# A residual norm by a product with a diagonal: three norms of a two-layer float32 kernel on Trainium2

## What is computed

```python
def rmsnorm(x, g):
    xf = x.astype(jnp.float32)
    y = xf * lax.rsqrt(jnp.mean(xf * xf, axis=-1, keepdims=True) + RMS_EPS)
    return (y * g.astype(jnp.float32)).astype(x.dtype)
...
    h = rms_norm(x, norm_mix_g)
    aq, ak, av, hq, hf, hi, hg, ga, gh = split_combined(h @ w_in)
...
    x = x + merged @ w_out
    x = x + peer_layer(rms_norm(x, norm_ffn_g), w_peer_q, peer_keys, peer_u, peer_v)
```

## Time and profile before

| | us |
|---|---|
| median of 3 runs | 1443.85 |
| lowest, highest | 1443.55, 1445.56 |
| the profiled execution | 1443.56 |
| its span, first to last instruction | 1441.8 |
| TensorE busy | 1422.6 |
| VectorE busy | 967.4 |
| ScalarE busy | 738.5 |
| GpSimd busy | 212.7 |

### The profile page before, as it was taken

The page is one execution under the profiler, slowest core; times in us unless marked ns, Lnnn a source line. Parts: engine busy times, 40 slices in busy tenths (PEclk is TensorE's granted clock), DMA queues, the critical chain, the costliest instruction groups (busy, mean ns, idle before and its releaser), DMA issues.

```text
span 1441.8 us, 25221 instructions
## 1 busy us (share of the span) xinstructions
PE 1422.6 (99%) x10281; PEld 1290.2 (89%) x10281; DVE 967.4 (67%) x1752; ACT 738.5 (51%) x1066; POOL 212.7 (15%) x122
## 2 busy tenths in 40 slices
PE   8999999999999999999999999999999999999997
PEld 7989989999999999998777778888899788899986
DVE  5565674693944777778888876655577864677754
ACT  5674654545454444444444445544567754655543
POOL 5000000488883000000000000000114100000000
PEclk9999999999999999999999999999999999999999
DMA  6433456455555545445545466555543453455552
GB/s 241 142 132 125 138 157 216 141 186 180 187 180 182 170 162 174 164 164 173 174 164 174 164 222 245 181 185 188 175 147 118 159 177 112 154 188 185 181 190 103
DMA packets 67219, 245.07 MB, mean 170 GB/s; under 512 B 7456, under 2 KB 7712, under 8 KB 66848
## 3 DMA queue, kind: packets, MB, share of 16 engines
q1 hardware_dynamic: 66960, 243.19, 50.5%
q10 hardware_dynamic: 144, 0.26, 0.0%
HBM read 242.37 MB, written 1.05 MB: 169 GB/s over the span
## 4 chain that ended last, share of the span: by engine, by line
PE 77%; issue 14%; DVE 4%; ACT 4%; POOL 1%; DMA 0%; POOLq 0%; SPq 0%; DVEq 0%; ACTq 0%
PE bank L433 76%; ACT A L1154 2%; DVE wlo L1712 1%; ACT whi L1154 1%; PE bank L442 1%; DVE A L1712 1%; ACT L1154 1%; DVE A L1708 0%; DVE xres L1712 0%; DMA xres<-in_x 0%; POOL wlo L2555 0%; ACT hTh L1154 0%; DVE small L2361 0%; DVE small L1712 0%; POOL small L2561 0%
## 5 line engine op out<-in xcount | busy, mean ns | idle before, releaser
L1712 DVE TENSOR_TENSOR wlo<-raw,whi 128x1024 fp32r<-128x1024 f32 (+1 forms) x375 | 458.1, 1223 | 334.3 <-ACT whi L1154 333.9
L1154 ACT ACTIVATE whi<-raw 128x1024 fp32r<-128x1024 f32 (+1 forms) x450 | 472.9, 1053 | 401.3 <-PE bank L433 401.3
L433 PE MATMUL bank<-hTh,whi 128*128 128x256 f32 x1944 | 555.5, 286 | 2.0 <-DVE wlo L1712 1.3
L433 PE MATMUL bank<-hTl,whi 128*128 128x256 f32 x1944 | 548.6, 282 | 0.0
L433 PE MATMUL bank<-hTh,wlo 128*128 128x256 f32 x1944 | 548.0, 282 | 0.0
L433 PEld LDWEIGHTS bank<-hTh,whi 128*128 128x128 f32 x1944 | 367.0, 189 | 5.9 <-DVE wlo L1712 2.1
L433 PEld LDWEIGHTS bank<-hTh,wlo 128*128 128x128 f32 x1944 | 366.0, 188 | 0.0
L433 PEld LDWEIGHTS bank<-hTl,whi 128*128 128x128 f32 x1944 | 365.5, 188 | 0.3 <-issue 0.2
L433 PE MATMUL bank<-whi,hTh 128*128 128x512 f32 (+2 forms) x552 | 218.4, 396 | 0.2
L433 PE MATMUL bank<-wlo,hTh 128*128 128x512 f32 (+2 forms) x552 | 215.0, 390 | 0.0
L433 PE MATMUL bank<-whi,hTl 128*128 128x512 f32 (+2 forms) x552 | 214.9, 389 | 0.0
(11 more groups left out here) (178 smaller groups left out, 1391.8 us busy)
## 6 DMA issues: line engine op xcount, KB each, us to landing
raw<-in_u SPq DMA_DIRECT2D x128, 512.0 KB, 3.3
raw<-in_v SPq DMA_DIRECT2D x128, 512.0 KB, 3.3
raw<-in_w_up SPq DMA_DIRECT2D x44, 512.0 KB, 3.3
raw<-in_w_down SPq DMA_DIRECT2D x22, 512.0 KB, 3.2
raw<-in_w_in_t SPq DMA_DIRECT2D x17, 512.0 KB, 3.4
raw<-in_w_in_g SPq DMA_DIRECT2D x16, 512.0 KB, 3.3
raw<-in_w_out SPq DMA_DIRECT2D x16, 512.0 KB, 4.0
raw<-in_w_pq SPq DMA_DIRECT2D x16, 512.0 KB, 3.5
```

Source lines behind the costliest of these rows:

```text
L433: return e.matmul(o, l, r, start=st, stop=sp_, skip_group_check=True)
L1154: return e.activation(o, i, func, **kw)
L1712: return e.tensor_tensor(o, a, b, op)
```

## The change

The scalings of the three norms go. In their place ScalarE writes `diag[:, 0:128]` = `ident` times the factor of block 0 (`diag0`) and VectorE `diag[:, 128:256]` for block 1 (`diag1`), and TensorE multiplies each 128x128 tile of `xres` itself, as the stationary operand, by that diagonal: the output is the tile transposed and scaled. ScalarE adds its two partial sums of block 1 itself (`n_part`), and VectorE adds the rest and the epsilon in one operation. On ScalarE the exponential for `h_kinv` moves one step later, and the logarithms of the recurrence's norm one step later, with what follows them; on VectorE the low part of `yhT` moves one step later. In cross attention the transposes of block 1 move from the step of block 0 to the middle of the next unit. At the end GpSimd multiplies first and takes both factors after. A line of "..." stands for context that is left out.

```diff
@@ -140,20 +140,20 @@
 PARTS = {0: 1, 3: 2, 4: 3}
-SCALED = (0, 6, 10, 18, 26, 34)
-SCALED0 = {1: 2, 5: 6}
+SCALED = (0, 0, 0, 8, 16, 24)
+HEADS = {0: 1, 1: 2, 5: 3}
 B_TAPS = (2, 0, 0, 3, 6, 7, 7, 6)
...
 hi lo_dve lo_pool w acc0 acc1 acc2 ev_act ev_dve
-n_sq n_sum n_rstd n_scaled n_scaled0 n_tr n_hi n_lo r_add r_part final half
+n_sq n_sum n_rstd n_scaled n_diag0 n_diag1 n_tr n_hi n_lo r_add r_part final half
 sig lb_dve lb_act at_bias at_pe at_act at_dve hi_ev hg_pe hg_act hg_dve mg_sum mg_hi mg_lo
...
 ff_a ff_c ff_g ff_h ff_lo
-own_act own_dve own_pool zeros x_sq hi_half lo_half lo_first f_xg f_xd f_act hd_mask
+own_act own_dve own_pool zeros x_sq hi_half lo_half lo_first f_xg f_xd f_act n_part hd_mask
 """.split()
@@ -212,6 +212,7 @@
         small = sb("small", 256)
+        diag = sb("diag", 2 * P)
         with ExitStack() as c:
@@ -467,37 +468,24 @@
-            def norm_tile(j, src, b, k):
-                if k % 2 == 0:
-                    if b == 0 and j in SCALED0:
-                        e.wait_ge(s["n_scaled0"], SCALED0[j] + k // 2 + 1)
-                    else:
-                        e.wait_ge(s["n_scaled"], SCALED[j] + (4 * b if j not in SCALED0 else 0) + k // 2 + 1)
+            def norm_tile(j, b, k):
+
+                if k == 0:
+                    e.wait_ge(s[("n_diag0", "n_diag1")[b]], HEADS[j])
                 o = (k // 4 * 2 + b) * P
-                ins = tr(banks[k % 4][:, o:o + P], src[:, b * D + k * P:b * D + (k + 1) * P])
+                ins = mm(banks[k % 4][:, o:o + P], xres[:, b * D + k * P:b * D + (k + 1) * P], diag[:, b * P:(b + 1) * P])
                 if b:
...
-            def first_head(src, spins):
-
-                def tile(b, k):
-                    if k % 2 == 0:
-                        if b == 0 and k < 4:
-                            e.wait_ge(s["n_scaled0"], k // 2 + 1)
-                        else:
-                            e.wait_ge(s["n_scaled"], k // 2 - 1 if b == 0 else 3 + k // 2)
-                    o = (k // 4 * 2 + b) * P
-                    ins = tr(banks[k % 4][:, o:o + P], src[:, b * D + k * P:b * D + (k + 1) * P])
-                    if b:
-                        ins.then_inc(s["n_tr"], 1)
+            def first_head(spins):
...
                 for k in range(8):
-                    tile(0, k)
+                    norm_tile(0, 0, k)
                 spin(spins[1], 7)
                 for k in range(4):
-                    tile(1, k)
+                    norm_tile(0, 1, k)
                 spin(spins[2], 7)
@@ -505,7 +493,7 @@
                     if k < 4:
-                        tile(1, k + 4)
+                        norm_tile(0, 1, k + 4)
                     if k == 4:
@@ -525,7 +513,7 @@
-            def norm_head(j, src, u0, spins):
+            def norm_head(j, u0, spins):
@@ -533,7 +521,7 @@
                             use(k)
-                        norm_tile(j, src, b, k)
+                        norm_tile(j, b, k)
                 bk = 4 + pair[0] % 3
@@ -543,7 +531,7 @@
                             if k < 4:
-                                norm_tile(j, src, 1, k + 4)
+                                norm_tile(j, 1, k + 4)
                         ins = three(banks[bk][:, 256 * i:256 * i + 256], [z[:, k, :] for z in wv],
@@ -958,6 +946,20 @@
+            def cross_turn(h2, b):
+                e.wait_ge(s["cr_dve"], 6 * h2 + 2 * b + 2)
+                use(2 + b)
+                for a in range(2):
+                    for q in range(2):
+                        ins = tr(banks[2 + b][:, (2 * a + q) * P:(2 * a + q + 1) * P],
+                                 p2[:, 2 * h2 + b, q, a * P:(a + 1) * P])
+                ins.then_inc(s["cr_pe"], 1)
+                free[2 + b] = (s["cr_act"], 6 * h2 + 3 + b)
+
+            def turn_mid(h2):
+                cross_turn(h2, 1)
+                yield
+
             def cross_mid(h2):
@@ -970,15 +972,8 @@
                     yield
-                    for b in range(TB):
-                        e.wait_ge(s["cr_dve"], 6 * h2 + 2 * b + 2)
-                        use(2 + b)
-                        for a in range(2):
-                            for q in range(2):
-                                ins = tr(banks[2 + b][:, (2 * a + q) * P:(2 * a + q + 1) * P],
-                                         p2[:, 2 * h2 + b, q, a * P:(a + 1) * P])
-                        ins.then_inc(s["cr_pe"], 1)
-                        free[2 + b] = (s["cr_act"], 6 * h2 + 3 + b)
+                    cross_turn(h2, 0)
+                    mid.lists[0].append(turn_mid(h2))
                     yield
@@ -995,7 +990,7 @@
             e.wait_ge(s["zeros"], 1)
-            first_head(scr, (15, 0, 1))
+            first_head((15, 0, 1))
             lin_T(BASE["w_in_t"] + 2, 2, hTv, KD)
@@ -1027,7 +1022,7 @@
-            norm_head(1, scr, BASE["w_pq"], (4, 1, 2))
+            norm_head(1, BASE["w_pq"], (4, 1, 2))
             lin_T(BASE["w_pq"] + 2, 14, hTv, KD)
@@ -1141,7 +1136,7 @@
             lin_A(BASE["w_xo"], oT2, KD, D, (4, 5, 6, 7), head_ready, split=3)
-            norm_head(5, xs, BASE["w_up"], (4, 1, 2))
+            norm_head(5, BASE["w_up"], (4, 1, 2))
             lin_T(BASE["w_up"] + 2, 42, hTv, KD)
@@ -1182,12 +1177,13 @@
                         accum_out=small[:, 4 * b + h:4 * b + h + 1]).then_inc(s["n_sq"], 1)
-
-            def scaled0(r, dst, n=4):
+                e.wait_ge(s["n_sq"], 4 * {0: 1, 3: 6, 4: 7}[r] + 2)
+                act(small[:, 9:10], small[:, 4:5], ACT.Identity, bias=small[:, 5:6]).then_inc(s["n_part"], 1)
+
+            def diag0(r):
                 e.wait_ge(s["n_rstd"], 2 * r + 1)
-                for c in range(n):
-                    act(dst[:, c * 256:c * 256 + 256], xres[:, c * 256:c * 256 + 256], ACT.Copy, scale=small[:, 2:3]
-                        ).then_inc(s["n_scaled0"], 1)
+                e.wait_ge(s_keep, 16)
+                act(diag[:, 0:P], ident, ACT.Copy, scale=small[:, 2:3]).then_inc(s["n_diag0"], 1)
@@ -1267,8 +1263,8 @@
                 act(eb, h_b, ACT.Exp).then_inc(s["hg_act"], 1)
+                yield
                 act(h_kinv, h_b, ACT.Exp, scale=-1.0).then_inc(s["hg_act"], 1)
-                yield
                 act(decay.unsqueeze(2), bl, ACT.Exp).then_inc(s["hg_act"], 1)
@@ -1499,7 +1496,7 @@
                 squares(xres, scr, b, 0)
-            scaled0(0, scr, 2)
+            diag0(0)
             e.wait_ge(s_w0, 16)
@@ -1556,7 +1553,7 @@
             part_squares(0, scr)
-            scaled0(1, scr)
+            diag0(1)
             hi(BASE["w_pq"] + 1)
@@ -1653,7 +1650,7 @@
             part_squares(3, xs)
-            scaled0(6, xs)
+            diag0(6)
             hi(BASE["w_up"] + 1)
@@ -1778,15 +1775,17 @@
                 again()
-                st = small[:, 4:8]
-                e.wait_ge(s["n_sq"], 4 * r + 2)
-                own(ts(small[:, 9:10], st[:, 0:1], st[:, 1:2], EPS, ALU.add, ALU.add))
-                again()
-                tt(st[:, 3:4], small[:, 8:9], small[:, 9:10], ALU.add).then_inc(s["n_sum"], 1)
+                e.wait_ge(s["n_part"], PARTS[at])
+                stt(small[:, 7:8], small[:, 8:9], EPS, small[:, 9:10], ALU.add, ALU.add).then_inc(s["n_sum"], 1)
+
+            def diag1(r):
+                e.wait_ge(s["n_rstd"], 2 * r + 2)
+                e.wait_ge(s_keep, 16)
+                ts(diag[:, P:2 * P], ident, small[:, 6:7], None, ALU.mult).then_inc(s["n_diag1"], 1)
...
                 part_add_and_sum(stage, b0, last, r, dst)
-                scaled(r, xres, dst, 1)
+                diag1(r)
@@ -2383,8 +2383,7 @@
                 rms_sum(0, b)
-            scaled(0, xres, scr, 0, (2, 3))
-            scaled(0, xres, scr, 1)
+            diag1(0)
             e.wait_ge(s["hi_half"], 1)
@@ -2605,7 +2604,7 @@
             rstd(1)
-            e.wait_ge(s["n_scaled"], 10)
+            e.wait_ge(s["n_diag1"], 2)
             lo(BASE["w_pq"] + 1)
@@ -2631,14 +2630,13 @@
             rstd(6)
-            e.wait_ge(s["n_scaled"], 38)
+            e.wait_ge(s["n_diag1"], 3)
             lo(BASE["w_up"] + 1)
             units(BASE["w_up"], 66)
-            rstd(7, (0,))
             e.wait_ge(s_gf2, 16)
...
             e.tensor_tensor(xg[:, D:D + 512], xres[:, D:D + 512], gfin2[:, 0:512], ALU.mult).then_inc(s["f_xd"], 1)
-            rstd(7, (1,))
+            rstd(7)
```

## The result

The changed kernel takes 1447.8 us (median of 8 runs, 1447.33 to 1448.64) against 1443.9 us for the kernel before (8 runs, 1443.29 to 1445.56): the ratio is 1.0026, with a 95% interval of 1.0017 to 1.0035. That is +3.9 us where +2.0 was forecast.

A forecast was written before the change was run, and what follows sets the result against it. TensorE's own work plus about 19 us of gaps bounds the kernel. 0.65 + 2.1 - 0.67 + 1.6 - 1.5 - 0.2 = +2.0 us gives 1445.9 us; forecast's own range 1444.8 to 1447.6, overall 1442.0 to 1447.9.

The forecast's parts named there:

- the rivals: Wait at w_ap goes (14%), tile costs a transpose (8%), both (5%), table load at Identity (5%), tile 0.44 us (3%).
- a longer chain at `w_ap` and slower handovers: ScalarE's chain before w_ap+2 and engine handovers: reasons for about 12 of the forecast's 65 points lying above 1446.7 us.
- first norm: Norm at the kernel's start: ScalarE and VectorE set the pace, diagonal tiles add 0.65 us, bounds 0.3 to 0.9.
- norm `w_pq`, norm `w_up`: Norms before w_pq and w_up: later first block and dearer tiles add about 1.05 us each, bounds +0.8 to +1.4.
- h_kinv's exponential: Chunked recurrence: exponential goes behind the weight split TensorE waits for, removing its 0.67 us idle at 104.07.
- logarithms, start of `w_ap`+2: Recurrence's end: old 1.76 us gap goes, TensorE waits 3.2 us at w_ap+2; net +1.5 to +1.6 us.
- cross attention: Second group of four transposes moves into the next unit, so TensorE's waits become products: -1.5 us, bounds -1.7 and 0.
- the end: Last norm: GpSimd multiplies first, block 1's factor comes earlier, ScalarE waits for factor 0: -0.2 us, bounds -0.5 and +0.3.
- the second move: Recurrence's logarithms moved from step 23 to 24: TensorE's wait shifts to w_ap+2, net +1.5 to +1.6 us.
- The price of a tile: Norms' diagonal product on TensorE: 0.22 us a tile against a transpose's 0.11, bounds 0.11 and 0.44.
- the rival of 0.44: Norms: a diagonal tile costs 0.44 us, transpose mode being 4 times faster for float32; 1455.2 us in all, 3%.
- the other reading: The end: by the shared-port rule the first factor would also wait for VectorE's squares, making this part +0.2 us.

The follow-up runs named there:

- after_filled: The changed kernel with 14 products of a zero tile on TensorE ahead of its wait for unit w_ap+2; 1446.09 us.
- before_filled: The kernel before with 7 products of a zero tile on TensorE ahead of its wait for unit w_ap+1, in its 1.76 us gap; 1443.58 us.
- before_late_logs: The kernel before with only the logarithms of the recurrence and the low part of yhT moved one step later; 1446.85 us, ratio 1.0017.
- norms_only_filled: The changed kernel with recurrence moves, cross attention split and end order put back, and 7 zero products ahead of w_ap+1; 1446.51 us.
- before_kinv_cross: The kernel before with only h_kinv's exponential one step later and cross attention's block 1 transposes in the next unit's middle; 1441.3 us, ratio 0.9981.

## Why the prediction was right, and where its size was off

The time, 1447.8, lies in the range that was given, 1442.0 to 1447.9, by 0.1 us and by luck: three of the eight runs are above it. It lies above the forecast's own 1444.8 to 1447.6, and the rise of 3.9 us is nearly twice the forecast one. The forecast called a rise of over 0.2% unlikely (20%); the measured 0.26% has an interval (0.17 to 0.35) on both sides of that. The mechanisms were those of the forecast, and none of the rivals came about. But one term was missing, and what the forecast allowed above 1446.7 was for a longer chain at `w_ap` and slower handovers, not for a clock. In us:

| term | forecast | measured | from |
|---|---|---|---|
| first norm | +0.65 | about +0.35 | start of unit 2, all profiles (below) |
| norm `w_pq`, norm `w_up` | +1.05 each | +1.37, +1.33 | traces |
| h_kinv's exponential | -0.67 | -0.70 | traces |
| logarithms, start of `w_ap`+2 | +1.6 | +1.69 | traces |
| lower clock behind the gap | none | +1.7 | changed, against after_filled |
| cross attention | -1.5 | -1.65 | traces |
| the end | -0.2 | about 0 | traces |

Without the clock the terms add to +2.4, and `after_filled` against `before_filled`, where no fall disturbs, is +2.5. No closer agreement can be asked of a sum that compares single executions. With 1.7 for the clock, 2.5 + 1.7 = +4.2 above the lower group of the kernel before (about 1443.6) is 1447.8. The kernel before pays for falls of its own in half of its runs; the median of its 8 runs, 1443.9, is a little above its lower group, and so the difference shown is 3.9.

- **The step that failed is the second move.** The forecast priced the longer gap by its start alone ("Net +1.5 to +1.6") and counted what follows at 0.12 us a product. The start was right to 0.1 us (169.6 forecast, 169.57 measured). TensorE did not come back at that speed: it took 0.21 us a product until about 172.4, and in `before_late_logs` until about 175. The nearest row was no help, since the 1.76 us gap in that profile had no fall behind it. A single profiled execution can miss an event that happens in half of them; the spread of the times shown, 1443.55 to 1445.56, was the only sign of it.
- **The price of a tile** was right: 0.23 us for 0.22, and 32 records for sixteen tiles, by the earlier trace rows. The transpose ran at 0.11 again, so the factor is 2, and the rival of 0.44 falls.
- **The norms** cost 0.3 more each. `diag0` came later: from the start of the squares to TensorE's first tile it is 0.75 us (211.54 to 212.29) where 0.61 was forecast. The eight tiles took 1.86 for 1.78, and the four between products added 0.51 for 0.45. (What the forecast calls the first full product at 212.36 is the transpose ahead of it; the product itself begins at 212.42. The comparison above takes the same row in both kernels.)
- **The first norm** was priced as if TensorE's tiles always set when it ends. In the profiled execution of the kernel before they and ScalarE's splits did. In `before_filled` ScalarE waited for the first weights, and that unchanged norm was slower than the changed one:

```profile
8.17 1.28 ACT L1156 ACTIVATE whi<-raw 128x512 fp32r<-128x512 f32 x2 [0.82 <-DMA raw<-in_w_in_t]
```

  The third unit begins at 17.06 to 17.81 in the six profiles with the old norm (mean 17.35) and at 17.63 to 17.86 in the seven with diagonals (17.70). The diagonals cost 0.35 on average and are hidden when the weights land late; `norms_only_filled` gives about 0.5.
- **The end** failed in its weighing only. VectorE's squares did get shorter (0.42 us where GpSimd's product was all but over, 0.98 in the old order), but ScalarE's wait for factor 0 took the whole gain. GpSimd's new order costs 0.24 us by the traces and 0.37 by the times, and the single small operation gains 0.24. So the end as a whole comes to between 0 and +0.13 (0.37 less 0.24), about midway between the -0.2 that the forecast took and the +0.2 that it gave as the other reading.

## What to carry to other kernels

Price a gap on TensorE by more than its length: ask at which clock the engine comes back, and where a wait cannot be removed, fill it with products into a free bank. Here seven such instructions brought the runs of the kernel before into one group (1443.19 to 1444.11). When run times fall into groups, find out to which group the profiled execution belongs before working out a sum from it. And moving a scaling from an engine with slack onto the engine that bounds the kernel has to be paid by the tile: here a plain float32 product of 128x128 took 0.23 us and a transpose 0.11, and there were 48 of them.

## What the runs showed of the hardware

The fall of TensorE's granted clock behind an idle stretch is a matter of odds: 0 of 11 runs at 1.10 us, 61 of 126 at 1.76 and 1.77, 6 of 11 at 1.92, 26 of 28 at 3.44 and 3.45. It cost about 1.5 us in the kernel before (between its groups) and 1.2 to 2.7 us in the changed one (its runs with a fall against 1446.1). In two profiled executions of the same gap of 1.76 us (the kernel before, and `before_kinv_cross`) one has a fall and the other has none. What distinguishes such executions was not tested, and stays open.
